# A hybrid decoder layer: the bias band laid out before the launch, attention's first operands staged one stage earlier, and routing scores with zero-padded keys issued a head ahead

## What is computed

```python
def _swa_attention(q, k, v, sinks, rel_bias):
    ...
    dist = qi + BLOCK - kj
    in_band = (dist >= 0) & (dist < WINDOW)
    ...
    bias = rel_bias[_t5_bucket(dist)].astype(jnp.float32)
    ...
    logits = logits + bias[None, None]
    logits = jnp.where(valid[None, :, None, None], logits, NEG)
...
def _fox_attention(q, k, v, log_f):
    ...
    F = jnp.transpose(jnp.cumsum(log_f, axis=1), (0, 2, 1))
    ...
        s = jnp.einsum('bqhd,bkhd->bhqk', qi, k).astype(jnp.float32) * (HEAD_DIM ** -0.5)
        s = s + Fi[..., :, None] - F[:, :, None, :]
...
def _peer(h, w_query, sub_keys, expert_down, expert_up):
    ...
        q = (xc @ w_query).reshape(T, PEER_HEADS, 2, PEER_HALF)
        s = jnp.einsum('thpd,hpkd->thpk', q, sub_keys).astype(jnp.float32)
        s1, i1 = lax.top_k(s[:, :, 0], PEER_TOPK)
        s2, i2 = lax.top_k(s[:, :, 1], PEER_TOPK)
```

## Time and profile before

| | us |
|---|---|
| median of 3 runs | 3811.93 (3811.81 to 3812.49) |
| the profiled execution | 3813.05, its span 3811.2 |
| `values` in the trace | 473.6 to 519.9 |
| first score of `attention` | 524.8 |
| DVE's first and last instruction of `routing` | 1074.4 and 1456.0 |

### The profile page before, as it was taken

How to read it: one execution, slowest core, us unless ns; L and a number is a source line. 1 busy time by engine, 2 the same in 40 slices (tenths; PEclk the granted TensorE clock), 3 DMA queues, 4 the chain that set the end, 5 groups by cost and what they waited for, 6 DMA issues and landing times. The chain is left out here.

```text
span 3811.2 us, 54409 instructions
## 1 busy us (share of the span) xinstructions
PE 3357.4 (88%) x17445; PEld 2831.7 (74%) x17445; DVE 2839.0 (74%) x5261; ACT 955.4 (25%) x1537; POOL 2123.5 (56%) x1285
## 2 busy tenths in 40 slices
PE   4999958888877779999998799999999999999985
PEld 3888646776665568888887687887878877878764
DVE  5111136652459998999998788888898888988999
ACT  3111135541222113333332122222222221221211
POOL 3990000014133335555555677777777777877876
PEclk8999979999988889999999899999999999999997
DMA  4443120014121111444443888888888888888886
GB/s 182 127 124 107 57 60 12 12 62 160 45 74 51 54 45 68 165 156 165 155 161 132 289 256 273 269 263 274 273 261 270 261 259 277 261 262 276 264 263 224
DMA packets 407622, 661.99 MB, mean 174 GB/s; under 512 B 219840, under 2 KB 273200, under 8 KB 404920
## 3 DMA queue, kind: packets, MB, share of 16 engines
q1 hardware_dynamic: 326520, 365.64, 30.2%
q0 software_dynamic: 78656, 286.30, 22.2%
q10 hardware_dynamic: 2304, 8.39, 0.5%
HBM read 563.75 MB, written 95.45 MB: 173 GB/s over the span
## 5 line engine op out<-in xcount | busy, mean ns | idle before, releaser
L376 PE MATMUL psum<-e_u_hi,e_w_hi 128*128 128x512 f32 x1536 | 612.6, 399 | 86.4 <-DVE acc L2214 59.7
L377 PE MATMUL psum<-e_u_lo,e_w_hi 128*128 128x512 f32 x1536 | 607.1, 395 | 0.0
L378 PE MATMUL psum<-e_u_hi,e_w_lo 128*128 128x512 f32 x1536 | 604.8, 394 | 0.0
L2214 DVE TENSOR_TENSOR acc<-acc,psum 128x512 f32<-128x512 f32 x756 | 474.3, 678 | 3.2 <-PE psum L378 3.0
L2224 DVE SCALAR_TENSOR_TENSOR acc<-e_row,e_row_weights_staged,acc 128x1024 f32<-128x1024 f32 x256 | 391.7, 1530 | 82.9 <-DMA e_row<-in_expert_up,rows_of 75.9
L2219 DVE SCALAR_TENSOR_TENSOR e_row<-e_row,h_rows 128x1024 f32<-128x1024 f32 x256 | 361.8, 1423 | 101.1 <-DMA e_row<-in_expert_down,rows_of 99.8
L2338 POOL DMA_INDIRECT e_row<-in_expert_down,rows_of x256 | 341.4, 1333 | 152.4 <-DVE e_row L2219 108.8
L2338 POOL DMA_INDIRECT e_row<-in_expert_up,rows_of x256 | 348.1, 1360 | 139.2 <-DVE acc L2224 94.8
L376 PEld LDWEIGHTS psum<-e_u_hi,e_w_hi 128*128 128x128 f32 x1536 | 293.4, 191 | 166.1 <-DVE acc L2214 58.7
L1871 POOL TENSOR_TENSOR g_hot<-g_hot,g_lo 128x512 fp32r<-128x512 bf16 x192 | 230.3, 1200 | 256.7 <-DVE g_hot L1839 256.7
L2349 POOL TENSOR_TENSOR e_u_lo<-e_up,e_u_hi 128x1024 fp32r<-128x1024 f32 x128 | 367.1, 2868 | 1.3
(11 more groups left out here) (268 smaller groups left out, 7815.8 us busy)
## 6 DMA issues: line engine op xcount, KB each, us to landing
e_up<-in_expert_up SPq DMA_DIRECT2D x128, 512.0 KB
gate_table<-g_table SPq DMA_DIRECT2D x12, 4096.0 KB, 12.4
e_table<-gate_table SPq DMA_DIRECT2D x128, 384.0 KB
e_left<-in_expert_downT SPq DMA_DIRECT2D x60, 512.0 KB
e_left<-gelus_ahead SPq DMA_DIRECT2D x68, 384.0 KB, 5.3
ga_downT<-in_expert_downT SPq DMA_DIRECT2D x48, 512.0 KB, 3.9
gelus_ahead<-ga_gelu SPq DMA_DIRECT2D x48, 384.0 KB
pw_raw<-in_w_in SPq DMA_DIRECT2D x34, 512.0 KB, 3.8
```

Source lines behind the costliest of these rows:

```text
L376: nc.tensor.matmul(out, l_hi(k), r_hi(k), start=k == 0, stop=False)
L377: nc.tensor.matmul(out, l_hi(k), r_lo(k), start=False, stop=False)
L378: mm = nc.tensor.matmul(out, l_lo(k), r_hi(k), start=False, stop=k == steps - 1)
L2214: nc.vector.tensor_tensor(out, out, m.psum[:, 2 + x % BANKS], ALU.add).then_inc(acc_d, 1)
```

## The change

- `line_constants()`, the input `line_const`, the matmul and the add of the line, the write of the line to DRAM and the eight reads are gone. `kernel()` lays the band out as an input `in_band` of 128 x 8 x 256 numbers (with `rel_bias` gathered by bucket and -1e30 outside the window), and SP reads it in one DMA of 128 rows of 8 KB.
- In `values` the forget sums stand behind the first two of the ten copies on DVE. SP writes `negF` to DRAM and reads its first two rows there. After the last transpose ACT stages the first queries, and POOL zeroes the halves and copies the first key chunk. The SP list ends on the four `kdup` DMAs and the band; DVE's last step waits for `negsink` alone. `attention` no longer has these steps.
- In `routing` the staged keys are 128 x 2 x 128 for a head: each half of the partitions holds its list in its own block and zero in the other (POOL clears the tile once, and ACT copies twice a head). One product of 128 rows and 256 columns gives both lists' scores of a tile, so a pair is two products, not four. Each pair has a PSUM bank of its own (4 to 7). Pairs 0 to 2 of head g + 1 are scored right behind `query(g + 1)`, and pair 3 at the head of `head(g + 1)`. Each pair waits until DVE has read the same pair of the head before.

```diff
-            sp.dma_start(t.line_dram, line[:].unsqueeze(1).to_broadcast([FOX_HEADS, P, LINE])).then_inc(wrote, 16)
-            sp.wait_ge(wrote, 16)
-            for h in range(FOX_HEADS):
-
-                src = bass.AP(t.line_dram.tensor, h * P * LINE + P - 1, [[LINE - 1, P], [1, 2 * P]])
-                sp.dma_start(t.band[:, h], src).then_inc(bands, 16)
-            sp.wait_ge(bands, 16 * (5 + FOX_HEADS))
+            sp.dma_start(t.negsink[:], a.sinks.partition_broadcast(P)).then_inc(sinks, 16)
+            sp.dma_start(t.band[:], a.band).then_inc(bands, 16)
+            sp.wait_ge(fv, 4)
+            sp.dma_start(t.negf_dram, t.negF[:]).then_inc(negf_out, 16)
+            sp.wait_ge(negf_out, 16)
+            for par in range(2):
+                sp.dma_start(t.nf[:, par], t.negf_dram[par:par + 1, :].partition_broadcast(P)) \
+                    .then_inc(t.negf_in[par], 16)
+            sp.wait_ge(bands, 16 * 5)
...
+            act.wait_ge(turned, 2 * len(vchunks))
+            for par in range(2):
+                rows = slice(par * HD, (par + 1) * HD)
+                nc.scalar.activation(first_q[par], t.qkvT[rows, 6], ACT.Copy, scale=SCALE).then_inc(t.q_fox, 1)
...
+            pool.wait_ge(turned, 2 * len(vchunks))
+            for par in range(2):
+                nc.gpsimd.memset(t.q_st[(1 - par) * HD:(2 - par) * HD, :, par], 0.0).then_inc(t.q_zero, 1)
+            pool.wait_ge(t.q_zero, 2)
+            nc.gpsimd.tensor_copy(t.k_st[:, 0], t.qkvT[:, 10]).then_inc(t.k_fox, 1)
...
+            def forget_sums():
+                dve.wait_ge(fv, 2)
+                dve.wait_ge(fx, 3)
+                nc.vector.tensor_tensor(fe[:], fe[:], fl[:], ALU.add).then_inc(fv, 1)
+                dve.wait_ge(fv, 3)
+                dve.wait_ge(fo, 1)
+                nc.vector.tensor_tensor_scan(t.negF[:], one[:], fe[:], 0.0, ALU.mult, ALU.add).then_inc(fv, 1)
+
             for n in range(len(vchunks)):
+                if n == 1:
+                    forget_sums()
...
-        return m.psum[:, 4 + 2 * ((i // 2) % 2) + s, (i % 2) * P:(i % 2 + 1) * P]
+        return m.psum[:, 4 + i // 2, (2 * (i % 2) + s) * P:(2 * (i % 2) + s + 1) * P]
...
             def score(g, u, pair):
                 if pair == 0:
-                    pe.wait_ge(kstaged, g + 1)
+                    pe.wait_ge(kstaged, g * 2 + 2)
                     pe.wait_ge(drained, g * UNITS + 2)
-                if not (isinstance(g, int) and g == 0 and pair < 2):
-
-                    pe.wait_ge(x1, g * 2 * TT + (4 * pair - 4))
-                    pe.wait_ge(l1, g * 2 * TT + (4 * pair - 4))
+                if not (isinstance(g, int) and g == 0):
+                    pe.wait_ge(x1, g * 2 * TT + (4 * pair + 4 - 2 * TT))
+                    pe.wait_ge(l1, g * 2 * TT + (4 * pair + 4 - 2 * TT))
                 for i in (2 * pair, 2 * pair + 1):
-                    for s in range(2):
-                        rows = slice(s * HD, (s + 1) * HD)
-                        mm = nc.tensor.matmul(score_at(i, s), qT[rows, u, i * P:(i + 1) * P], kst[rows, u],
-                                              start=True, stop=True)
+                    both = m.psum[:, 4 + pair, (i % 2) * 2 * P:(i % 2 + 1) * 2 * P]
+                    mm = nc.tensor.matmul(both, qT[:, u, i * P:(i + 1) * P], kst[:, u].rearrange("p s k -> p (s k)"),
+                                          start=True, stop=True)
                 mm.then_inc(scored, 1)
 
             def head(g, u):
                 unit = g * UNITS + 2
-                score(g, u, 0)
-                score(g, u, 1)
+                score(g, u, 3)
                 ahead_half(g * 2, 0, 0, unit)
-                score(g, u, 2)
                 ahead_half(g * 2, 0, 1, unit + 1)
-                score(g, u, 3)
                 ahead_half(g * 2 + 1, 1, 0, unit + 2)
                 ahead_half(g * 2 + 1, 1, 1, unit + 3)
                 if not last(g):
                     query(g + 1, 1 - u, unit + 4)
+                    for pair in range(3):
+                        score(g + 1, 1 - u, pair)
             query(0, 0, 0)
+            for pair in range(3):
+                score(0, 0, pair)
...
-                nc.scalar.activation(kst[:, u], kT[:, g], ACT.Copy).then_inc(kstaged, 1)
+                for s in range(2):
+                    rows = slice(s * HD, (s + 1) * HD)
+                    nc.scalar.activation(kst[rows, u, s], kT[rows, g], ACT.Copy).then_inc(kstaged, 1)
```

More of the change, by code:

```diff
@@ L76, in bucket_of_line, with band_bias @@
     return np.where(d < exact, d, np.minimum(large, BUCKETS - 1)).astype(np.int32), ok
-def line_constants():
+def band_bias(rel_bias):
     bucket, ok = bucket_of_line()
-    c = np.zeros((BUCKETS + 1, LINE), np.float32)
-    for m in range(LINE):
-        if ok[m]:
-            c[bucket[m], m] = 1.0
-        else:
-            c[BUCKETS, m] = NEG
-    return c
+    at = P - 1 - np.arange(P)[:, None] + np.arange(2 * P)[None, :]
+    rows = np.concatenate([rel_bias, np.full((1, rel_bias.shape[1]), NEG, np.float32)])[np.where(ok, bucket, BUCKETS)]
+    return np.ascontiguousarray(rows[at].transpose(0, 2, 1))
 class Memory:
@@ L570, in values @@
     fo = m.sem("v_forget_ones")
-    pick = m.at("v_pick", [BUCKETS, LINE], 178)
-    outside = m.at("v_outside", [FOX_HEADS, LINE], 180)
-    rel = m.at("v_rel", [BUCKETS, FOX_HEADS], 182)
-    line = m.at("v_line", [FOX_HEADS, LINE], 183)
-    small = m.sem("v_small")
     turned = m.sem("v_turned")
     copied = m.sem("v_copied")
-    lined = m.sem("v_lined")
-    linec = m.sem("v_line_copied")
-    wrote = m.sem("v_line_written")
     bands = m.sem("v_bands")
+    sinks = m.sem("v_sinks")
+    negf_out = m.sem("v_negF_out")
+    first_q = [t.q_st[par * HD:(par + 1) * HD, 0, par] for par in range(2)]
     vchunks = [5, 14, 15, 16, 17]
@@ L636, in _ @@
             nc.vector.tensor_scalar(fl[:], z, t.bfl[:, 0:1], None, ALU.add).then_inc(fv, 1)
-            dve.wait_ge(lined, 1)
-            dve.wait_ge(small, 48)
-            nc.vector.tensor_tensor(line[:], m.psum[0:FOX_HEADS, 7, 0:LINE], outside[:], ALU.add) \
-                .then_inc(linec, 1)
             dve.wait_ge(fv, 1)
@@ L763, in load @@
                 sp.dma_start(nf[:, par], row.partition_broadcast(P)).then_inc(negf_in[par], 16)
-            sp.dma_start(t.negf_dram, t.negF[:]).then_inc(negf_out, 16)
-            sp.wait_ge(negf_out, 16)
-            for par in range(2):
-                load(0, par)
             with sp.Fori(0, PAIRS - 1) as i:
@@ L775, in _ @@
         def _(pool):
-            for par in range(2):
-                nc.gpsimd.memset(q_st[(1 - par) * HD:(2 - par) * HD, :, par], 0.0).then_inc(q_zero, 1)
-            pool.wait_ge(q_zero, 2)
-            nc.gpsimd.tensor_copy(k_st[:, 0], t.qkvT[:, 10]).then_inc(k_fox, 1)
             def pair(i, last):
@@ L893, in pair @@
                         stage(0, i + 7, q_fox)
-            stage(0, 6, q_fox)
             for j in range(AHEAD_S):
@@ L1722, in head @@
                     chosen(g - 1)
+            nc.gpsimd.memset(kst[:], 0.0).then_inc(kzeroed, 1)
             rest(0, 0)
@@ L2387, with __init__ @@
 class Arrays:
-    def __init__(self, args, line_const):
+    def __init__(self, args, band):
         self.x = args["x"]
```

56 lines of the change are left out of this document (22 added, 34 removed).

## The result

The changed kernel took 3763.05 us (median of 4 runs, 3762.36 to 3768.69) beside 3812.21 us before: ratio 0.9873 [0.9856, 0.989], 49 us less. The forecast was 3742 with a range to 3760. The profiled execution of it took 3768.69 us (span 3766.9), the longest of its four. Each ratio is against its own group's; a difference of a few us between two groups is read from the stages and not from the medians.

What follows compares the result with a forecast made beforehand. `values` was taken as bound by the band's load outside the engines, `routing` by DVE with waits for scores. Gains of 31.7 + 19.9 + 1.3 + 15 + 1.7 = 69.6 us off 3811.93 gave 3742.3, range 3735 to 3760.

Steps and rivals of the forecast that it cites:

- the sum: Whole kernel: gains of 31.7 + 19.9 + 1.3 + 15 + 1.7 = 69.6 us, taken off the median 3811.93, give 3742.3.
- `values`, 31.7 us: Stage `values`: without the wait for the band, PE's first attention score comes at 493.1 instead of 524.80, 31.7 us less.
- `routing`, 19.9 + 1.3 + 15: Stage `routing`: 19.9 us from DVE's waits for scores, 1.3 from head 1's wait, 15 from DVE steps stretched beside POOL.
- The six waits: `routing`, heads 2 on: DVE's six waits for PE's scores all go, 31.0 - 11.05 = 19.9 us.
- the surplus: `routing`: extra time of DVE steps where POOL works, 21 us in all; 15 us should go, bounds -3 and 19.
- The estimate for a padded pair of scores: `routing`, PE: two padded products of 256 columns take about 0.7 us at most, against 0.72 a pair before.
- The stage's end, 1.7 us: End of `routing`: PE's tail ends some 9 us before DVE's, the stage 0.8 us after DVE; 1.7 us gained.
- Attention to norm: Stretch from PE's first attention score to DVE's first `routing` step: forecast at 549.6 us, the same as before.
- A: `routing`: DVE's meetings with POOL stay, at other places; gain 54.6 us, 3757; chance 0.2.
- B: `values`: the band's load or SP's list replaces the wait; gain there 20 instead of 31.7, 3754; chance 0.08.
- C: `routing`: ACT holds PE, so scores ahead come too late; only 31.7 + 1.3 = 33 us gained, 3779; chance 0.06.
- D: `routing`: PE becomes the bound, its clock staying at the lower level; slower by 55 us, 3867; chance 0.04.

Runs made afterwards that it cites:

- the run with 192 in the first stage: Changed kernel plus 192 PE instructions of satisfied waits in the program's first stage, behind PE's first product, none at the start of `experts`: 3746.49 us, ratio 0.9823.
- late staging: Changed kernel plus 192 idle PE instructions at the start of `experts`, with POOL's clearing, first keys and queries and `negF` trip back in `attention`: 3752.05 us.

## Why the prediction was wrong, step by step

- **The step that failed** is the sum: "all terms are differences inside the trace, so they are taken off the median". It holds only if the stages behind stay as they are, and no rival said otherwise. The change shortened PE's code by some 192 instructions, the blocks of it fell onto the gathers of `experts`, and 18 us came back there (1637.0 in place of 1619.1). With the code's position restored and nothing paid for it (the run with 192 in the first stage) the change as it is took 3746.5 us, 68.4 less than the kernel before in its group, where 69.6 were forecast. So near a match is partly luck, since terms that missed both ways stand in it.
- **`values`, 31.7 us**: 29.9 (53.2 - 23.3). The wait for the band went, and what came next was what had been named. Two sizes were short. The last transposes ended at 489.8, where the forecast, moved by the 1.1 us by which P came later, has 488.6. Its own terms (484.3 + 4 x 0.61 + 2 x 0.6) give 487.9 and not the 487.5 that it used; and PE, which had idled 6.30 us, made the last four units in 3.67 us, 0.92 each and not 0.6, at a granted clock of 0.50 from 486 to 490 us. And from POOL's last step to the first score lie 1.4 us, not 0.9. The credit was wrong: nearly all of the gain is the band's and the earlier scan's together, which no run tells apart; the early staging has 0.5 of it at most.
- **`routing`, 19.9 + 1.3 + 15**: 35.4 of 36.2 (379.3 - 343.9). The six waits went; head 1 waits 9.00 in place of 11.05, 2.0 us. Of the surplus, that of L1647 and L1645 went whole (6.2 and 4.1 us), that of L1667 by 42.2 - 38.1 = 4.1, and L1603's did not: all 64 of them took 13.8 us (277 ns in the mean) before and 14.5 (286) after, the 336 of the earlier trace rows being that of the 32 of 64 columns alone. That is 13.7 of the 15. The estimate for a padded pair of scores, 0.7 us at most, was low: four pairs took 3.69 us at full clock, 0.92 each, which PE's slack covers. But the prediction argued from the new order of PE's list, and the old order on four banks keeps all but 4 us. It saw that PE idled 12.6 us for a shared bank, and did not ask what the banks alone would do. Here the size was right with the credit in the wrong place.
- **The stage's end, 1.7 us**: 0.8 in the stretch to the first sum.
- **Attention to norm**, taken as unchanged, shows 2.8 us more after. Its length is 547.8 to 552.8 in these runs, without a pattern by kernel (547.8 is the kernel before with 64 instructions, 549.6 the one without). What sets it was not tried. P, likewise, came at 467.1 to 472.8 in stages that are the same in all but two of the runs; what moves it is open, and one trace of each kernel can't tell whether the same kernel differs from itself as much.
- **Rivals.** A (3757) and B (3754) are nearest in time, but neither happened: L1627 is at 0.29, and no wait for the band is left. C and D did not happen either. The range ended at 3760 since nothing in it stood for a stage that the change doesn't touch.

## What to carry to other kernels

A change of the instruction count of an engine with long loops moves where its code blocks are read in every loop behind it; if a stage that was not touched becomes longer and its work, clock and bytes have not changed, compare first passes of its loops with later ones, and try the same kernel with some dozens of idle instructions more on that engine before explaining anything else. When a wait goes, ask which half of the edit took it, the order or the buffers: here the old order on separate banks kept all but 4 us, and on shared banks lost 39. A step moved ahead gains nothing while it still waits for the same last event; splitting it by what each part waits for gave 4 us where moving it gave half of one.

## What the runs showed of the hardware

- PE's code came in blocks of 16 KB on queue 8, of the kind "instruction": about one in 26 us in the first pass of a loop whose pass is some 104 us long, and none in the later passes, but for one near the end of some loops. In the pass of chunks 32 to 39 a wait for gathered rows with a block read 2 to 6 us ahead of it was 4.1 to 4.7 us long, where most others were 2.7 to 3.4; the gathers ahead of the first of these waits were issued at the same point of the pass (13.6 us). Adding idle instructions to PE's list alone brought the long waits (3829.3 beside 3812.1 us) or took them away (3746.5 beside 3763.1). That the block's packet, some 1.1 us long, stands ahead of row packets on a DMA engine fits in size; which engine carries it isn't in the traces, so this last link is argued, not shown.
- Instructions that hold nothing but satisfied waits are not free on PE: 192 of them made an idle stretch of 25.43 us out of one that was 19.58 with 128 of them, so they take up to 25.43 / 192 = 0.13 us each.
- DVE's multiply of 128x8 took 1.25 us in place of 0.17 when it came 0.6 us into POOL's first clearing, and 0.16 with no clearing beside it (late staging). The Trainium skill says of the port pair that DVE and GpSimd share that it is an exclusive lock for a whole instruction (SBUF — State Buffer, SBUF: two separate sides); the size agrees, since it ends at 491.70 and the first of the two clearings, 3.66 / 2 = 1.83 us from 489.86, at 491.69.
